# Small 32-bit matmuls split over TensorE's two column halves, and compression blocks built in two parts

## The reference

```python
def compress(kv, pos, w1, w2):          # blocks of 32 tokens, every 16 tokens: 15 blocks
    idx = jnp.arange(n_cmp)[:, None] * CMP_STRIDE + jnp.arange(CMP_BLOCK)[None, :]
    blocks = kv[:, idx] + pos[None, None, :, None, :]
    return jax.nn.gelu(blocks @ w1) @ w2

# sliding-window attention, selected-block attention and window attention, 8 heads of 64 each:
logits = einsum('bqgrd,bkgd->bgrqk', q, k) * scale + bias
out = einsum('bgrqk,bkgd->bqgrd', softmax(logits), v)
# compressed attention: the same with 15 compressed keys and values per group, bias head_bias(table, dist_c)
# retention: o = o * rsqrt(mean(o * o, axis=-1) + EPS) per head of 128
```

## Time and profile before

| | us |
|---|---|
| median of 3 timed runs | 869.11 |
| lowest and highest | 868.76, 869.61 |
| the profiled execution | 869.88 |
| its span | 867.8 |
| TensorE matmuls busy | 853.3 |
| TensorE weight loads busy | 756.7 |
| VectorE busy | 643.1 |
| ScalarE busy | 446.9 |
| GpSimd busy | 73.3 |

### The profile page before, as it was taken

One profiled execution on the slowest core, in us unless ns is written; L12 is line 12 of the kernel. 1 busy time (PEld: TensorE's weight loads), 2 busy tenths in 40 slices (PEclk: granted clock), 3 DMA queues, 4 the chain that ended last, 5 costly groups with the idle time before them and its releaser, 6 DMA issues.

```text
span 867.8 us, 13655 instructions
## 1 busy us (share of the span) xinstructions
PE 853.3 (98%) x5253; PEld 756.7 (87%) x5257; DVE 643.1 (74%) x812; ACT 446.9 (51%) x567; POOL 73.3 (8%) x64
## 2 busy tenths in 40 slices
PE   8999999999999999999999999999999999999995
PEld 6888888889998888888888999889998988888894
DVE  5776775767867686766775867877766788898897
ACT  6444444445333645444445545576434655665663
POOL 1100000004230200000003300200003000000000
PEclk9999999999999999999999999999999999999998
DMA  8876566556744477665566653745546456456441
GB/s 255 302 240 193 175 203 201 159 179 211 226 146 120 134 251 249 215 220 193 169 192 167 154 161 107 204 116 134 192 146 194 146 166 218 149 195 219 167 170 48
DMA packets 119232, 158.08 MB, mean 182 GB/s; under 512 B 4572, under 2 KB 104332, under 8 KB 119068
## 3 DMA queue, kind: packets, MB, share of 16 engines
q1 hardware_dynamic: 116460, 150.93, 55.1%
q0 software_dynamic: 1488, 5.34, 1.7%
q10 hardware_dynamic: 1248, 1.32, 0.5%
HBM read 154.79 MB, written 1.07 MB: 180 GB/s over the span
## 4 chain that ended last, share of the span: by engine, by line
PE 80%; DVE 11%; issue 5%; ACT 2%; DMA 1%; ACTq 0%; DVEq 0%
PE acc L1751 20%; PE wk L1652 20%; PE wk L1621 20%; PE wk L1660 11%; DVE w_lo L961 3%; DVE work L1522 2%; PE wk L2055 2%; DVE work L1512 1%; ACT work L740 1%; PE acc L2026 1%; DVE work L1509 1%; PE acc L2038 1%; PE acc L1668 1%; DMA x<-in_x 1%; ACT sq L765 1%
## 5 line engine op out<-in xcount | busy, mean ns | idle before, releaser
L1652 PE MATMUL wk<-xhl,w_hi 128*128 128x512 f32 x992 | 240.2, 392 | 0.0
L961 DVE TENSOR_TENSOR w_lo<-raw,w_hi 128x2048 fp32r<-128x2048 f32 x83 | 190.0, 2289 | 65.0 <-ACT w_hi L469 63.8
L1652 PEld LDWEIGHTS wk<-xhl,w_hi 128*128 128x128 f32 x992 | 183.3, 189 | 35.9 <-ACT w_hi L492 0.2
L1621 PE MATMUL wk<-xhl,w_hi 128*128 128x256 f32 x896 | 162.5, 287 | 0.1
L469 ACT ACTIVATE w_hi<-raw 128x2048 fp32r<-128x2048 f32 x83 | 158.1, 1905 | 0.0
L1751 PE MATMUL acc<-w_hi,hhl 128*128 128x512 f32 x480 | 153.3, 390 | 0.0
L462 ACT ACTIVATE w_hi<-raw 128x2048 fp32r<-128x2048 f32 x56 | 106.5, 1910 | 65.8 <-PE wk L1621 49.2
L1621 PEld LDWEIGHTS wk<-xhl,w_hi 128*128 128x128 f32 x896 | 137.3, 191 | 1.2 <-issue 0.7
L1660 PEld LDWEIGHTS wk<-xhl,w_lo 128*128 128x128 f32 x992 | 130.2, 192 | 6.4
L944 DVE TENSOR_TENSOR w_lo<-raw,w_hi 128x2048 fp32r<-128x2048 f32 x49 | 114.4, 2337 | 25.1 <-ACT w_hi L462 24.9
L1660 PE MATMUL wk<-xhl,w_lo 128*128 128x256 f32 x992 | 131.8, 283 | 0.0
(11 more groups left out here) (261 smaller groups left out, 962.1 us busy)
## 6 DMA issues: line engine op xcount, KB each, us to landing
raw<-in_ffn_w SPq DMA_DIRECT2D x65, 1024.0 KB, 5.3
raw<-in_w_in SPq DMA_DIRECT2D x26, 1024.0 KB, 6.8
raw<-in_w_ffn_in SPq DMA_DIRECT2D x22, 1024.0 KB, 5.1
raw<-in_w_ffn_out SPq DMA_DIRECT2D x11, 1024.0 KB, 4.9
raw<-in_w_out SPq DMA_DIRECT2D x8, 1024.0 KB, 4.9
arena<-bias_scratch POOLq DMA_DIRECT2D x4, 512.0 KB, 6.3
raw<-in_cmp_w_k SPq DMA_DIRECT2D x2, 1024.0 KB, 5.6
raw<-in_cmp_w_v SPq DMA_DIRECT2D x2, 1024.0 KB, 7.2
```

The lines of the kernel that those rows point to most:

```text
L961: nc.vector.tensor_tensor(w_lo[:, s], raw[:, s], w_hi[:, s].bitcast(F32), ALU.subtract) \
L1621: mm = nc.tensor.matmul(dst, w, v, start=start and n == 0, stop=stop and n == len(pairs) - 1, skip_group_check=True)
L1652: mm = nc.tensor.matmul(bank, wh[:, c, cols], xhl[:, c].rearrange("p n t -> p (n t)"), start=c == 0, stop=False, skip_group_check=True)
```

## The change

Each of the four groups of small 32-bit matmuls is issued as twice as many instructions. The first takes stationary columns 0 to 63 and writes partitions 0 to 63 of the result, the second takes columns 64 to 127 and writes partitions 64 to 127 (`for t0 in (0, HD)`, HD = 64). Both use the same moving operand. Semaphores are counted by the last instruction of a group, as before. `blocks` takes the index v (keys or values) and does four of the eight additions: v = 0 in unit 5, v = 1 in unit 6, each behind that position's attention work on VectorE, in place of both in unit 7. ScalarE waits for a count of two in place of one.

```diff
@@ -688,7 +688,7 @@
                     if (m, half) == (3, 1):
                         key_halves(0)
                     if (m, half) == (7, 1):
-                        act.wait_ge(blk_ready, 1)
+                        act.wait_ge(blk_ready, 2)
                         nc.scalar.activation(blk_hl[0], blk, ACT.Copy).then_inc(blk_hi, 1)
                     if (m, half) == (8, 0):
                         key_halves(1)
@@ -1329,20 +1329,19 @@
                     dve.wait_ge(y_taken, 2 * r + 2 - b)
                     step(nc.vector.tensor_tensor(y_b[:, b], y_b[:, b], y_tmp, ALU.add))
 
-            def blocks():
+            def blocks(v):
 
                 dve.wait_ge(cmp_in, 16 * 2)
                 dve.wait_ge(blk_zero, 1)
-                for v in range(2):
-                    for g in range(2):
-                        for s in range(2):
-                            rows = slice(HD * s, HD * (s + 1))
-                            src = kf[rows, K_CK + v] if g == s else cmp_turned[rows, v]
-                            src = bass.AP(tensor=src.tensor, offset=src.offset + s,
-                                          ap=[list(src.ap[0]), [2, 16], [16, NCMP]])
-                            pos = vec[rows, V_POSK + 16 * v:V_POSK + 16 * (v + 1)]
-                            last = nc.vector.tensor_tensor(blk[rows, v, :, g * 16:g * 16 + NCMP], src,
-                                                           bcast_in(pos, NCMP), ALU.add)
+                for g in range(2):
+                    for s in range(2):
+                        rows = slice(HD * s, HD * (s + 1))
+                        src = kf[rows, K_CK + v] if g == s else cmp_turned[rows, v]
+                        src = bass.AP(tensor=src.tensor, offset=src.offset + s,
+                                      ap=[list(src.ap[0]), [2, 16], [16, NCMP]])
+                        pos = vec[rows, V_POSK + 16 * v:V_POSK + 16 * (v + 1)]
+                        last = nc.vector.tensor_tensor(blk[rows, v, :, g * 16:g * 16 + NCMP], src,
+                                                       bcast_in(pos, NCMP), ALU.add)
                 last.then_inc(blk_ready, 1)
 
             def y_lo_part(n):
@@ -1444,8 +1443,8 @@
                         attend(k)
                     if half and m:
                         lo(U_IN2 + m + 2)
-                    if (m, half) == (7, 0):
-                        blocks()
+                    if (m, half) in ((5, 0), (6, 0)):
+                        blocks(m - 5)
                     if (m, half) == (8, 0):
                         dve.wait_ge(blk_hi, 1)
                         nc.vector.tensor_tensor(blk_hl[1], blk, blk_hl[0].bitcast(F32), ALU.subtract) \
@@ -1906,8 +1905,9 @@
                 for b in range(2):
                     for g in range(4):
                         y0 = OH_D0 + P * b - 64 * g - 31
-                        mm = nc.tensor.matmul(acc[:, 3, P * b + 32 * g:P * b + 32 * (g + 1)], oh4[:, y0:y0 + P],
-                                              table_diag, start=True, stop=True)
+                        for t0 in (0, HD):
+                            mm = nc.tensor.matmul(acc[t0:t0 + HD, 3, P * b + 32 * g:P * b + 32 * (g + 1)],
+                                                  oh4[:, y0 + t0:y0 + t0 + HD], table_diag, start=True, stop=True)
                 mm.then_inc(bias_cmp_mm, 1)
 
             pe.wait_ge(const_set, 3)
@@ -1973,8 +1973,10 @@
                         for h in range(HR):
                             for tt in range(2):
                                 n = 2 * h + tt
-                                mm = nc.tensor.matmul(wk[:, 2, n:n + 1], o_sq[:, h, tt * P:(tt + 1) * P],
-                                                      mean_h[:], start=True, stop=True)
+                                for t0 in (0, HD):
+                                    toks = slice(tt * P + t0, tt * P + t0 + HD)
+                                    mm = nc.tensor.matmul(wk[t0:t0 + HD, 2, n:n + 1], o_sq[:, h, toks], mean_h[:],
+                                                          start=True, stop=True)
                         mm.then_inc(hms_ready, 1)
                 if m == 8:
                     pool_mix(0)
@@ -2048,13 +2050,15 @@
                         nh, h0, b = (2, 2 * w, 1) if w < 4 else (4, 4 * (w - 4), 0)
                         for h in range(nh):
                             head = h0 + h
-                            dst = wk[:, 3 - b, head * HD:(head + 1) * HD]
+                            cols = slice(head * HD, (head + 1) * HD)
                             g = head // 4
                             for kc in range(b + 1):
                                 n = h * (b + 1) + kc
-                                mm = nc.tensor.matmul(dst, prob_t[s % 2][:, n * P:(n + 1) * P],
-                                                      v2[r % 2][:, kc, g * HD:(g + 1) * HD], start=kc == 0,
-                                                      stop=kc == b)
+                                for t0 in (0, HD):
+                                    mm = nc.tensor.matmul(wk[t0:t0 + HD, 3 - b, cols],
+                                                          prob_t[s % 2][:, n * P + t0:n * P + t0 + HD],
+                                                          v2[r % 2][:, kc, g * HD:(g + 1) * HD], start=kc == 0,
+                                                          stop=kc == b)
                         mm.then_inc(pv_mm, 1)
 
             def turn_values(n, bank):
@@ -2165,9 +2169,10 @@
                         for b in range(2):
                             for j in range(4):
                                 g = j // 2
-                                mm = nc.tensor.matmul(acc[:, 2, b * P + 32 * j:b * P + 32 * (j + 1)],
-                                                      qb_s[:, j, b * P:(b + 1) * P], kcz[:, :, g * 16:(g + 1) * 16],
-                                                      start=True, stop=True)
+                                for t0 in (0, HD):
+                                    mm = nc.tensor.matmul(acc[t0:t0 + HD, 2, b * P + 32 * j:b * P + 32 * (j + 1)],
+                                                          qb_s[:, j, b * P + t0:b * P + t0 + HD],
+                                                          kcz[:, :, g * 16:(g + 1) * 16], start=True, stop=True)
                         mm.then_inc(cscore_mm, 1)
                     if at == (19, 0):
                         pe.wait_ge(cprob, 1)
```

## The result

The kernel after took 862.78 us (median of four executions, 862.38 to 863.41); the kernel before, run again beside it, 869.08 us: -6.3 us, ratio 0.9932 with a 95% interval of 0.9921 to 0.9944. The forecast was 859.6 us, -9.5. The sign and the range held; a third of the gain is missing, and part of what is there does not come from where the forecast had it.

A forecast was written before the change was run, and what follows sets the result against it. TensorE was taken to bound the kernel, busy 853.3 of 867.8 us, its small 32-bit products paced by weight loads. -10.6 (halves) + 0.3 (ends) + 1.6 (waits) - 0.8 (blocks) = -9.5 us, giving 859.6; range 857.5 to 869.5.

The forecast's parts named there:

- The saving per record: Weight loads of the four split groups: a pair of halves costs 0.056 us, saving 0.055 on each of 192 records, 10.6 us.
- the reasoning from the row halves of L2026: Four loads there take 0.30 us, not 0.52, so two run together; column halves were taken to do the same.
- The ends of the stretches: At the ends of 21 stretches one half may trail the other: 0 to 1.1 us lost, taken as 0.3.
- The rival with 6.9 us for the modes: Each of 21 stretches pays 0.33 us for entering and leaving 64-column mode: 866.5 or 876.1 us; chance 0.10.
- Taken back by waits: Value products that come earlier wait longer for the ScalarE and VectorE chain: 1.6 us lost, bounds 0.7 to 3.0.
- The last value group: Value products at 595.12 us, their copy done 0.8 us before: 0.3 us allowed as taken back there.
- The blocks: Additions moved from unit 7 to units 5 and 6: TensorE's 0.8 us wait before the key transposes (L2063) goes.
- the likeliest case's range: Whole kernel, halves loading side by side: 857.8 to 863 us; chance 0.60.
- the bounds of the terms: Whole kernel, from the limits on saving per record, stretch ends and time taken back: 857.8 to 862.4 us.
- the allowance up to 863: Whole kernel: a mix with more waits taken back, up to 863 us, counted as part of the forecast.
- One half after the other: Split groups: the two halves load in turn, a pair costs 0.108 to 0.118 us, 869.2 in all, no change; chance 0.18.
- The clock: Near 25 us: the shorter bias products also remove the low-clock stretch, another 1.5 us, 858.1 in all; chance 0.12.

## Why the prediction was right, and where it was off

- *The saving per record.* Forecast 0.055 us of 192 records, 10.6. Measured 0.111 - 0.058 = 0.053, 10.2. Pairs start together, and the reasoning from the row halves of L2026 held.
- *The ends of the stretches.* This term failed. It stood at 0.3 us in the sum and measured 5.1 (10.2 less the 5.1 that reached the groups behind, slot 9 taken like its neighbours), 0.24 us in each of 21. I had the right row, the 0.33 us around L2142, and set it aside because L2106 and L2108 change columns without a gap. But those are fp32r and the groups that were split are 32-bit; the rows print both as f32, and the difference stands in the code. So the sentence that the trace bears out the drained array for fewer rows and not for fewer columns was a false reading: it is the type that tells them apart. The rival with 6.9 us for the modes was nearer in this term than the forecast; I gave it 0.10. Its place was right, its price too high where a group of 64 rows stands straight ahead and the array runs empty anyway: there a stretch costs 0.15, behind transposes 0.33.
- *Taken back by waits.* Forecast 1.6 (up to 3.0), measured 0.9 (0.6 and the 0.3 that slot 9's own group gains), half before its transposes, half before its products, through ScalarE's high half and L636 as described. It is smaller because the value groups ahead gained less. The last value group gave nothing back. One wait was missed: the bias products, said to be followed by units that had been ready for microseconds, are followed 11 us later by the chain of L462 and L1060, which has 0.2 us to spare. It took 0.8 back in the profile after, all of their 0.69.
- *The blocks.* Forecast 0.8, measured 0.9 at the key transposes. The additions stand four and four at 511 and 520 us and delay nothing. Unforeseen: 1.0 us from the stop in VectorE's loop.
- *Sum.* -10.2 + 5.1 + 0.9 - 0.9 - 1.0 = -6.1, and -5.3 with the 0.8 at 35 us, against -6.3 measured (interval -4.9 to -6.9, which holds both; a low clock that comes less often with the split would add to either). That the time fell inside the likeliest case's range was luck in part. Errors of opposite sign met: 4.8 us too little for the ends and, the other way, a stop of 1.0 us that nobody had seen. And 862.78 lies outside the 862.4 that the bounds of the terms gave; only the allowance up to 863 holds it.
- *Rivals.* One half after the other: false, a pair takes 0.059 us. The clock: its price right (1.5 forecast, 1.56 in the ledger), its cause open, since the low stretch comes and goes with the bias products in one piece and may be rarer with them split. The mode: true for 32-bit matmuls, at 5.1 us for 6.9, and not for fp32r.

## What to carry to other kernels

Splitting a 32-bit matmul over the column halves halves its cost only within a long run of such matmuls: price each way in and out of the run (here 0.15 to 0.35 us), and put runs of the same tile size side by side where what they need is ready. When a row is used as evidence for another instruction, check that the type is the same in the code, and not only the shape. When two profiles differ far behind the change, look there for a wait that is not of the change before crediting the change with it. And follow a gain to the next place where another engine's chain meets TensorE: here it was met 11 us behind the bias products.

## What the hardware showed that I had not expected

- The second 64-column half of a pair is free with 64 moving columns or one: 16 loads and matmuls of L2058 in 0.55 us, 8 in 0.54; 32 of the means in 1.01.
- A change of the number of stationary columns lets the array run empty for 32-bit matmuls (0.13 us for one change at 256 moving columns; for in and out 0.19 at 1 and 0.35 around 64 to 128) and not for fp32r ones (0.115 us from load to load between 32, 64 and 128 columns).
- One instruction more on VectorE, ahead of a loop, took 0.37 us out of the first turn inside the loop and 0.12 out of each later one: 1.0 us at the end of the kernel.
- The low granted clock near 25 us (0.50, a cost of 1.56 us) came in the profiles of two kernels and not in those of two others with the same work up to there.
